# First stage of a two-layer kernel reordered by tiles of tokens, with the values' weights first

## What is computed

```
n = rmsnorm(x, g_mix)                      # 256 x 1024
proj = n @ w_in                            # q, k_c, v_c, k_s, v_s, gates, ...
k_cmp = compress(k_c, ...)                 # blocks of 32 tokens, gelu MLP
v_cmp = compress(v_c, ...)
o = nsa_attention(q, k_cmp, v_cmp, k_s, v_s, k_w, v_w)
```

```
bias_by_dist = rel_bias[t5_bucket(arange(S))]   # 4 heads, by distance
s = s + bias                                    # in diff_attention
```

## Time and profile before

| | before |
|---|---|
| median of 3 runs | 746.71 us |
| span of the profiled execution (first to last instruction) | 745.2 us |
| PE busy | 740.4 us (99%) |
| DVE busy | 518.0 us (70%) |
| ACT busy | 416.4 us (56%) |
| POOL busy | 66.5 us (9%) |

### The profile page before, as it was taken

One profiled execution on the slowest core, in us unless ns is written; L12 is line 12 of the kernel. 1 busy time (PEld: TensorE's weight loads), 2 busy tenths in 40 slices (PEclk: granted clock), 3 DMA queues, 4 the chain that ended last, 5 costly groups with the idle time before them and its releaser, 6 DMA issues.

```text
span 745.2 us, 11582 instructions
## 1 busy us (share of the span) xinstructions
PE 740.4 (99%) x4563; PEld 641.4 (86%) x4563; DVE 518.0 (70%) x834; ACT 416.4 (56%) x788; POOL 66.5 (9%) x103
## 2 busy tenths in 40 slices
PE   9999999999999999999999999999999999999998
PEld 8999999877888888888888888887888888888886
DVE  5784677885756678887367757898667777447762
ACT  5575557556463455565356546597646656345640
POOL 6300000000010000430000004400100000000000
PEclk9999999999999999999999999999999999999999
DMA  8998444343455546766656461735355655656611
GB/s 266 297 311 274 85 109 153 114 128 123 146 170 197 167 152 222 198 213 228 188 172 212 171 226 54 251 124 174 111 168 170 191 204 174 222 170 188 207 57 56
DMA packets 99209, 131.26 MB, mean 176 GB/s; under 512 B 5357, under 2 KB 79163, under 8 KB 99156
## 3 DMA queue, kind: packets, MB, share of 16 engines
q1 hardware_dynamic: 96564, 125.58, 52.6%
q0 software_dynamic: 2304, 4.43, 2.7%
q10 hardware_dynamic: 288, 0.52, 0.2%
HBM read 128.68 MB, written 1.84 MB: 175 GB/s over the span
## 4 chain that ended last, share of the span: by engine, by line
PE 97%; DVE 2%; ACT 1%; issue 0%; POOL 0%; POOLq 0%
PE B L1626 39%; PE B L1592 22%; PE B L1597 11%; PE B L1581 11%; PE B L1805 2%; PE B L1852 2%; PE B L1815 2%; PE B L1639 1%; PE B L1685 1%; PE B L1633 1%; DVE LO L1002 1%; PE B L1808 1%; PE B L1832 1%; PE B L1730 1%; PE B L1791 0%; PE B L1729 0%
## 5 line engine op out<-in xcount | busy, mean ns | idle before, releaser
L1002 DVE TENSOR_TENSOR LO<-RAW,HI 128x1024 fp32r<-128x1024 f32 x236 | 282.5, 1236 | 101.0 <-ACT HI L538 100.5
L1626 PE MATMUL B<-HI,AA 128*128 128x512 f32 (+1 forms) x960 | 286.8, 376 | 0.3 <-DVE AA L1008 0.2
L538 ACT ACTIVATE HI<-RAW 128x1024 fp32r<-128x1024 f32 (+1 forms) x240 | 237.2, 1038 | 63.1 <-PE B L1626 58.2
L1626 PEld LDWEIGHTS B<-HI,AA 128*128 128x128 f32 x960 | 175.7, 188 | 33.8 <-issue 1.6
L1592 PE MATMUL B<-AA,HI 128*128 128x512 f32 x704 | 179.2, 393 | 0.0
L1626 PE MATMUL B<-LO,AA 128*128 128x512 f32 (+1 forms) x480 | 178.6, 372 | 0.0
L1592 PEld LDWEIGHTS B<-AA,HI 128*128 128x128 f32 x704 | 126.8, 189 | 23.0 <-issue 0.7
L1626 PEld LDWEIGHTS B<-LO,AA 128*128 128x128 f32 x480 | 90.6, 189 | 14.6
L1597 PEld LDWEIGHTS B<-AA,LO 128*128 128x128 f32 x704 | 96.6, 190 | 7.1
L1597 PE MATMUL B<-AA,LO 128*128 128x256 f32 x704 | 98.8, 282 | 0.0
L1581 PE MATMUL B<-AA,HI 128*128 128x256 f32 x448 | 83.3, 287 | 0.0
(11 more groups left out here) (313 smaller groups left out, 634.9 us busy)
## 6 DMA issues: line engine op xcount, KB each, us to landing
RAW<-in_w_in SPq DMA_DIRECT2D x29, 1024.0 KB, 5.8
RAW<-in_w_gate SPq DMA_DIRECT2D x22, 1024.0 KB, 5.3
RAW<-in_w_up SPq DMA_DIRECT2D x22, 1024.0 KB, 5.3
RAW<-in_w_down SPq DMA_DIRECT2D x22, 1024.0 KB, 5.0
RAW<-in_w_in SPq DMA_DIRECT2D x10, 512.0 KB, 6.4
RAW<-in_w_attn_out SPq DMA_DIRECT2D x4, 1024.0 KB, 5.1
RAW<-in_w_o SPq DMA_DIRECT2D x4, 1024.0 KB, 5.0
RAW<-in_w_out SPq DMA_DIRECT2D x4, 1024.0 KB, 5.0
```

Source lines behind the costliest of these rows:

```text
L538: e.activation(pieces(HI, NSPL, i, k), pieces(RAW, NRAW, i, k), ACT.Copy).then_inc(split_hi, 1)
L1002: e.tensor_tensor(pieces(LO, NSPL, i, k), pieces(RAW, NRAW, i, k), pieces(HI, NSPL, i, k), ALU.subtract).then_inc(split_lo, 1)
L1626: x = e.matmul(dst, a, w[:, t, c0:c0 + n], start=(first and t == 0 and k == 0), stop=(last and t == nk - 1 and k == 2))
```

## The change

It does the following:

- Unit 0 is now the values' weights of the selection branch (before, unit 12); the keys' weights become unit 1, and the units 1 to 11 of before become 2 to 12. From unit 13 on nothing is renumbered.
- The first unit is multiplied with the activations stationary, tile of tokens by tile, each in quarters (`quarter`: tile t, half h, 4 products of 256 columns). All of tile 0 that needs only its own rows stands ahead of the turning of tile 1.
- Tile 0 has its own mean and its own root on POOL, and so has tile 1; ACT no longer scales tile 1, DVE does.
- x's first half goes by ACT's queue, the gain row is SP's first DMA, x's second half of tile 0 SP's second.
- `idle` is called with 9, 6 and 1 in place of 14, 13 and 3.
- The bias table's inputs are loaded right after the first root, its product stands between tile 0's and tile 1's first products, into bank 4. Its move to DRAM also waits for the last queries (`q_sb` 8).
- The keys' unit is then an ordinary one (`keys(U_KEYS, 0, c)`), which waits for both halves of its low part.
- In the attention of the first block one piece of `fill()` now goes ahead of the first scores, and one behind them.

The diff, cut to its core:

```diff
         w1 = A["w_in"][0]
         QO, KO, GBO = 1536, 2560, 4096
+        cols(w1, KO + 768, 256, vals_pe, 2)
         cols(w1, KO + 512, 256, keys_pe, 2)
...
-        cols(w1, KO + 768, 256, vals_pe, 2)
...
         @block.sync
-            for h in range(2):
-                e.dma_start(X[:, 0, halves(h)], A["x"][0, 0:128, halves(h)]).then_inc(x_in[h], 16)
-                if h == 0:
-                    e.dma_start(GAIN[0:128:64, :], A["g_mix"][0, :].rearrange("(a n) -> a n", a=2)).then_inc(row_in, 16)
+            e.dma_start(GAIN[0:128:64, :], A["g_mix"][0, :].rearrange("(a n) -> a n", a=2)).then_inc(row_in, 16)
+            e.dma_start(X[:, 0, halves(1)], A["x"][0, 0:128, halves(1)]).then_inc(x_in[1], 16)
...
         @block.gpsimd
-            e.dma_start(VR[46:47, :], A["gla_gate_b_2"]).then_inc(rows_in, 16)
             e.wait_ge(setup, HALF)
-            root(1, ST[:, 6:8], ST[:, 4:6])
+            root(1, ST[:, 6:7], ST[:, 4:5], 1)
+            e.dma_start(OH[:, :], A["c_onehot"]).then_inc(rel_in, 16)
+            e.dma_start(REL[0:32, :], A["rel_bias_2"]).then_inc(rel_in, 16)
+            e.wait_ge(root_sb, 1)
+            e.memset(REL[32:33, :], NEG).then_inc(setup, 1)
+            e.wait_ge(setup, FAR)
+            root(2, ST[:, 7:8], ST[:, 5:6], 1)
+            e.dma_start(VR[46:47, :], A["gla_gate_b_2"]).then_inc(rows_in, 16)
...
             e.wait_ge(rel_sb, 1)
+            e.wait_ge(q_sb, 8)
             e.dma_start(bias_rows.rearrange("h r n -> h (r n)").rearrange("h (r n) -> h r n", n=ROW),
...
         @block.scalar
+            e.dma_start(X[:, 0, halves(0)], A["x"][0, 0:128, halves(0)]).then_inc(x_in[0], 16)
...
-            for t, h in ((0, 0), (1, 0), (0, 1)):
-                e.wait_ge(x_in[2 * t + h], 16)
-                squares(2 * t, X[:, t, :], QK[:, t, :], h)
+            e.wait_ge(x_in[0], 16)
+            squares(0, X[:, 0, :], QK[:, 0, :], 0, squares0_sb)
+            e.wait_ge(x_in[2], 16)
+            squares(2, X[:, 1, :], QK[:, 1, :], 0, squares_sb, 2)
             hi(0, 0)
-            e.wait_ge(root_sb, 1)
-            for h in range(2):
-                e.wait_ge(gained_sb, 2 + h)
-                e.activation(TOK[:, 1, halves(h)], TOK[:, 1, halves(h)], ACT.Copy, scale=ST[:, 7:8]).then_inc(scaled_act, 1)
...
+            turned(0, B[5], 0, 0)
+            turned(1, B[6], 4, 0)
             hi(0, 1)
+            turned(2, B[5], 0, 1)
+            turned(3, B[6], 4, 1)
             hi(1)
+            values(0, 0)
+            hi(2)
+            values(0, 1)
+            e.wait_ge(rel_pe, 1)
+            e.activation(OH[0:4, :], B[4][0:4, 0:ROW], ACT.Copy).then_inc(rel_sb, 1)
             keys(0, 0)
...
         @block.vector
+            second_square(0).then_inc(squares0_sb, 1)
+            e.wait_ge(squares0_sb, 2)
+            mean(0).then_inc(mean_sb, 1)
             e.wait_ge(gain_pe, 1)
...
+            e.wait_ge(x_in[0], 16)
+            own.step(e.tensor_tensor(TOK[:, 0, halves(0)], X[:, 0, halves(0)], B[2][:, :], ALU.mult))
+            e.wait_ge(root_sb, 1)
+            own.wait()
+            e.tensor_scalar(TOK[:, 0, halves(0)], TOK[:, 0, halves(0)], ST[:, 6:7], None, ALU.mult).then_inc(scaled_sb, 1)
+            normed(0, 1)
+            second_square(1).then_inc(squares_sb, 2)
             e.wait_ge(squares_sb, 4)
+            mean(1).then_inc(mean_sb, 1)
+            turned(0, B[5], 0, 0)
             lo(0, 0)
+            turned(1, B[6], 4, 0)
+            e.wait_ge(root_sb, 2)
+            for h in range(2):
+                e.wait_ge(x_in[2 + h], 16)
+                normed(1, h)
             lo(0, 1)
+            turned(2, B[5], 0, 1)
+            turned(3, B[6], 4, 1)
             lo(1)
+            lo(2)
...
         @block.tensor
+            first_turn(0)
+            first_turn(1)
+            idle(1)
+            take(0, vals_sb, 1)
+            e.wait_ge(split_hi, 1)
+            e.wait_ge(turn_hi, 1)
+            quarter(0, 0, AH, hi, True)
+            e.wait_ge(turn_lo, 1)
+            quarter(0, 0, AL, hi)
+            e.wait_ge(split_hi, 2)
+            e.wait_ge(turn_hi, 2)
+            quarter(0, 1, AH, hi)
+            unit_ready(U_VALS, 0)
+            quarter(0, 0, AH, lo)
+            e.wait_ge(turn_lo, 2)
+            quarter(0, 1, AL, hi)
+            e.wait_ge(rel_in, 32)
+            e.wait_ge(setup, FAR)
+            take(4, rel_sb, 1)
+            e.matmul(B[4][0:4, 0:ROW], REL[:, :], OH[:, :], start=True, stop=True).then_inc(rel_pe, 1)
+            first_turn(2)
+            first_turn(3)
...
+            for c in range(2):
+                keys(U_KEYS, 0, c)
...
-            for t in range(2):
-                values(U_VALS, 0, t)
...
+            filler = fill()
+            next(filler)
             e.wait_ge(q_sb, 8)
...
-                for _ in range(FILL_AT[i]):
+                for _ in range(FILL_AT[i] - (i == 0)):
                     next(filler)
```

More of the change, by code:

```diff
@@ L1045, in _, with mean, second_square @@
-            lo(0, 0)
-            for t in range(2):
-                turned(t, B[5 + t], 0, t)
+            def mean(t):
+                return e.scalar_tensor_tensor(ST[:, 4 + t:5 + t], ST[:, 2 * t:2 * t + 1], EPS, ST[:, 2 * t + 1:2 * t + 2],
+                                              ALU.add, ALU.add)
+            def second_square(t):
+                e.wait_ge(x_in[2 * t + 1], 16)
+                return e.scalar_tensor_tensor(QK[:, t, halves(1)], X[:, t, halves(1)], 1.0 / 1024, X[:, t, halves(1)], ALU.mult,
+                                              ALU.mult, accum_out=ST[:, 2 * t + 1:2 * t + 2])
@@ L1641, in _ @@
             e.wait_ge(setup, ONE)
-            idle(14)
+            idle(9)
             e.wait_ge(row_in, 16)
@@ new lines, in _, with quarter @@
+            hi, lo = view(HI, U_VALS), view(LO, U_VALS)
+            def quarter(t, h, a, w, first=False, last=False):
+                d = slice(t * 128, t * 128 + 128)
+                for c in range(4 * h, 4 * h + 4):
+                    x = e.matmul(B[t][:, 0:256], a[:, c, d], w[:, c, :], start=(first and c == 0), stop=(last and c == 7))
+                return x
+            first_turn(0)
[3 more added lines that the diff above has]
+            e.wait_ge(split_hi, 1)
@@ new lines, in _ @@
+            first_turn(2)
+            first_turn(3)
+            take(1, vals_sb, 2)
+            e.wait_ge(turn_hi, 3)
+            quarter(1, 0, AH, hi, True)
+            quarter(1, 0, AH, lo)
+            unit_ready(U_VALS, 1)
+            quarter(0, 1, AH, lo, last=True).then_inc(vals_pe, 1)
+            e.wait_ge(turn_hi, 4)
+            quarter(1, 1, AH, hi)
+            quarter(1, 1, AH, lo)
+            for h in range(2):
+                e.wait_ge(turn_lo, 3 + h)
+                x = quarter(1, h, AL, hi, last=True)
@@ L1776, in _ @@
             queries(3, 1)
-            for t in range(2):
-                values(U_VALS, 0, t)
-            e.wait_ge(setup, FAR)
-            take(0, rel_sb, 1)
-            e.matmul(B[0][0:4, 0:ROW], REL[:, :], OH[:, :], start=True, stop=True).then_inc(rel_pe, 1)
             def scores(s):
```

163 lines of the change are left out of this document (56 added, 107 removed).

## The result

| | before | after |
|---|---|---|
| median, same chip, 5 runs each | 746.71 us (746.63 to 748.02) | 749.31 us (748.07 to 749.72) |
| span of the profiled execution | 745.2 us | 747.3 us |
| PE busy | 740.4 us | 737.6 us |
| DVE busy | 518.0 us | 519.0 us |
| ACT busy | 416.4 us | 414.6 us |

What follows compares the result with a forecast made beforehand. PE was taken to bound the kernel nearly everywhere, with DVE setting the end of the ramp. Ramp +5.8, removal -6.6 and stall +1.8 gave +1.0 us on the median of 746.71: 747.7 us, range 744.8 to 749.8 us.

Steps and rivals of the forecast that it cites:

- The stall: Third filler piece (values) in the attention: PE waits for ACT's copy of keys(1, 0), +1.8 us, bounds 0 and 2.9.
- The removal: Further down, 67.00 to 73.58 us: values' products and bias product no longer made there, -6.6 us.
- The start of the chain: Ramp: DVE can start the first turned part at about 11.0 us, decided by the weights' landing; norm allows 9.4 us.
- rival A: Ramp as fast as the norm allows, DVE starting at 9.4 us, stall stays: 746.4 us; chance 0.13.
- The landing of x: Start of the ramp: x's second half, second on its queue, lands near 5.4 us, taking 4.0 us.
- Rival C: Ramp: x's half lands late and the bias inputs hold PE, 0.9 to 1.5 us more, 749.1 us; chance 0.14.
- The chain: Ramp: DVE's turned parts, low halves and scalings from 11.0 us through unit 1's low halves, ending at 19.9 us.
- The time outside the span: Whole kernel: median 746.71 us lies 1.5 us above the profiled span of 745.2 us; forecast added to the median.
- The smaller idle counts: Ramp: fewer idle products counted at nothing, since PE waits for data anyway.
- B: Rival, faster: ramp as in case A and no stall, ACT in time or PE with hidden slack, 744.6 us; chance 0.16.
- D: Rival: PE falls to slower pace after ramp gaps, keys' 48 products cost +3.9 us, 751.6 us; chance 0.04.
- E: Rival: stall and ramp as forecast, but units 5 to 12 come late, 1 to 2 us more, 749 us; chance 0.06.

Runs made afterwards that it cites:

- The experiment on the kernel before: Kernel before with one edit: the first filler piece goes ahead of the first scores; 749.35 us, ratio 1.0031.
- both changes: Changed kernel with both filler pieces behind the first scores again and the bias product behind the values; 747.12 us, ratio 1.0004.

## Why the prediction was right and wrong

The stall and the sum of what goes and comes were right, the ramp was counted too short: 747.7 us was said and 749.31 us measured. That is inside the range, but no longer within the 1.5 us (0.2%) of the kernel before that the prediction called no change; the ratio's interval begins at 1.002. The miss of 1.6 us is three terms: 0.95 us in the ramp, 0.14 us at the stall, and 0.5 us outside the span.

- **The removal, -6.6 us.** It held. The ramp gave +6.75 us against it, where +5.8 us was said: the small transposition behind the first units stands at 26.62 us, before at 19.87 us. Less the 6.58 us that went out of the earlier trace rows, 0.17 us is left at the beginning of the attention, and the rest of the 2.11 us arises behind it.
- **The stall, +1.8 us.** It held in place, cause and size: 2.11 - 0.17 = 1.94 us by the timelines, 1.8 us by the table. ACT's copy of keys stood behind two high halves, as said. The experiment on the kernel before showed it with the old first stage, and the one with the high halves first took it away.
- **The stretch of 20 to 67 us, 0.** It held. No wait is recorded there.
- **The start of the chain, 11.0 us.** It was 10.29 us. The weights' first half landed 0.9 us earlier than in the earlier trace rows. By itself that was a part of rival A, a gain. The norm, said to be ready for 9.4 us and 1.6 us early, was in fact 0.16 us later than the weights. (The gain product was said to end near 6.7 us. The working's own terms, 1.06 + 3.65 + 1.13 us, give 5.8 us, and 5.83 us was measured; nothing hung on it, since x came later.)
- **The landing of x, "near 1.4 + 4.0 = 5.4 us".** This is the step that failed. Of two rows it took the one of ACT's queue, 4.0 us, for a transfer on SP's queue, where 5.8 us stood; measured were 5.2 us to landing, and 6.70 us on the clock. Rival C was worked out from the right row and named the right limit (a mean at 7.2 us; it came at 7.44), and got 0.14. Its price, 0.9 to 1.5 us, is what the table shows: 10.4 against 9.15 to 9.5 us. Had x landed at 5.4 us, 1.3 us earlier, the inputs would by the same steps have been there near 13.4 us, just before PE: an estimate from the rows above. No run had x early with the product in its place, so that x alone removes the wait is worked out, not shown; early inputs do remove it, as the experiment with them shows.
- **The chain, 8.9 us with the bias product in it.** Without a wait it measures 9.15 to 9.5 us, so it was 0.3 to 0.6 us short too.
- **The time outside the span, 1.5 us.** That compared a median with the span of another execution. In single runs, time less span was 1.7 to 1.8 us for the kernel before and 1.9 to 2.0 us for the changed one. The kernel before with the piece ahead still has 1.7 to 1.8 us, so the 0.2 us more do not come from the order at the attention; which other part of the change they come from was not tried and stays open.
- **The smaller idle counts, at nothing.** In the changed kernel this was right, and the test without any shows why: its cover is the wait for the bias inputs. With the counts of before the median is 0.4 us higher, too little to tell. (Of the 27 calls in the first two batches 12 are gone, of all 30 calls 14; the prediction's 13 of 30 is neither.)
- **Rivals.** C's mechanism came, with A's early weights beside it. B did not: ACT was not in time. D did not come in the changed kernel. Half clock behind gaps of PE did come in the ramp of three versions, but in each it was over before the keys' products, which D had priced. E did not.

## What to carry to other kernels

When work is moved into a gap of the beginning, ask what its inputs are queued behind: here a product of 0.7 us, moved ahead of the turning on an engine that works in order, made everything behind it wait for a load of 0.5 KB. When a piece of work is moved ahead of another on one engine, look at which order the engines that empty its banks keep; moving the matching two instructions on ACT took the whole stall away. And subtract the start of the last unchanged stretch from each span: it sorts a dozen runs that differ by tenths of a per cent into the part that an edit changed and the part that the first microseconds change by themselves.

## What was not expected of the hardware

- The pace of PE in its first microseconds changes to about twice the speed at another time in each profile, from about 0.23 us for a recorded idle product (18 of them in 4.14 us, start to start, in the version with the bias product late) to 0.12 us (26 in 3.20 us in the earlier trace rows). The 0.20 us that the prediction read from the earlier trace rows is a mean over both. The change came before 6.7 us in the earlier trace rows, before 4.7 us in the changed kernel, and at 10, 10 to 11 and 12 us in three of the versions, two of which have the same instructions of PE ahead of it. The granted clock reads 1.00 all along, although the pace is that of half clock: four products take 1.05 us here (no idle products, 13.08 us) and 1.05 us at a granted 0.50 (both changes, 12.87 us). Twenty recorded idle products in a row ended with the slow pace still on for most of them; the one version without any kept it longest, until nearly 14 us. So whether idle products bring the time forward stays open, and so does what sets it. A slow start goes with a long run in the version with the inputs early, whose profile is one of the three of 747.7 us; for the spread of 2 to 4 us in the other versions it is a likely part, not a shown one.
- Apart from that, the granted clock does fall to 0.50 (1.2 GHz; 1.00 is 2.4 GHz) in the profiles of three versions, behind gaps of PE of 0.6 us (one of 1.1 us shortly before it), 1.6 us and 5.7 us. The low clock stands in the rows from 10:12 to 14:16 us after the short gaps, and from 16:18 to 26:28 us after the long one. The prediction's sentence that the trace shows no return is about the kernel before, and holds for it. The Trainium skill ("TensorE: Matmul & The Clock Gate", Part 1), by which idle time takes the clock back, agrees with the gap of 5.7 us. The short gaps it does not sort: two of them are followed by the low clock, while gaps of 1.6 us in the changed kernel, of 1.9 us in the version with the bias product late, of 3.1 us in the version without idle products and of 1.0 and 0.8 us in the version with the high halves first show a clock of 1.00 behind them, so the length of a gap alone does not tell which comes.
- The first transfers land at other times in each execution: x's half on SP's queue at 6.1 to 7.6 us when second, at 4.3 us when first; the weights' first half at 8.4 to 9.7 us. A chain that depends on two of them has a spread of a microsecond from that alone.
